# RWKV-7 chunk solve in a decoder trunk: two 64-row halves solved one after the other instead of one 128-row inverse

## What is computed

```python
def step(S, inp):
    r_t, w_t, k_t, v_t, kk_t, a_t = inp
    sa = jnp.einsum('bhij,bhj->bhi', S, -kk_t)
    S = (S * w_t[:, :, None, :]
         + sa[..., None] * (kk_t * a_t)[:, :, None, :]
         + v_t[..., None] * k_t[:, :, None, :])
    y = jnp.einsum('bhij,bhj->bhi', S, r_t)
    return S, y
```

## Time and profile before

| | us |
|---|---|
| median of 3 runs (1505.07 to 1511.18) | 1505.27 |
| the profiled execution, as a whole | 1507.26 |
| its span, first to last instruction | 1505.4 |
| TensorE busy | 1474.2 |
| VectorE (DVE) busy | 1242.6 |
| ScalarE (ACT) busy | 1009.8 |

### The profile page before, as it was taken

The page is one execution under the profiler, slowest core; times in us unless marked ns, Lnnn a source line. Parts: engine busy times, 40 slices in busy tenths (PEclk is TensorE's granted clock), DMA queues, the critical chain, the costliest instruction groups (busy, mean ns, idle before and its releaser), DMA issues.

```text
span 1505.4 us, 22041 instructions
## 1 busy us (share of the span) xinstructions
PE 1474.2 (98%) x8088; PEld 1226.9 (82%) x8088; DVE 1242.6 (83%) x1375; ACT 1009.8 (67%) x1157; POOL 22.2 (1%) x19
## 2 busy tenths in 40 slices
PE   8999999999899999999999999999999999999997
PEld 5888888799798588888888888888888888888885
DVE  3756666787885289999999999999999999999997
ACT  2544444663523178888888888888888878888885
POOL 0000000000000020000000000000000000000200
PEclk9999999999999999999999999999999999999998
DMA  9889553036405499999999999999999999999990
GB/s 361 326 271 301 175 168 112 1 117 217 141 2 178 174 322 372 395 392 395 396 392 396 394 368 388 390 365 383 394 366 373 393 386 362 395 380 362 349 369 28
DMA packets 206696, 453.57 MB, mean 301 GB/s; under 512 B 8881, under 2 KB 46257, under 8 KB 206386
## 3 DMA queue, kind: packets, MB, share of 16 engines
q1 hardware_dynamic: 203154, 446.12, 80.6%
q0 software_dynamic: 1280, 4.20, 1.1%
q10 hardware_dynamic: 2208, 2.50, 0.5%
HBM read 437.58 MB, written 23.60 MB: 306 GB/s over the span
## 4 chain that ended last, share of the span: by engine, by line
PE 92%; DVE 5%; ACT 2%; DMA 1%; issue 0%; DVEq 0%; ACTq 0%
PE psum L1591 20%; PE psum L1593 20%; PE psum L1592 20%; PE psum L2401 5%; PE psum L2404 3%; PE psum L902 2%; PE psum L2325 2%; PE psum L2365 2%; PE psum L2366 2%; PE psum L2367 2%; PE psum L600 2%; PE psum L1609 2%; PE psum L2318 1%; PE psum L696 1%; DVE time_mix_parts L1150 1%; PE psum L722 1%
## 5 line engine op out<-in xcount | busy, mean ns | idle before, releaser
L1799 DVE TENSOR_TENSOR w_lo<-ring,w_hi 128x1024 fp32r<-128x1024 f32 x672 | 811.0, 1224 | 63.5 <-ACT w_hi L1693 15.8
L1693 ACT ACTIVATE w_hi<-ring 128x1024 fp32r<-128x1024 f32 x672 | 711.3, 1062 | 172.5 <-PE psum L1593 172.4
L1591 PE MATMUL psum<-w_hi,xg_split 128*128 128x512 f32 x896 | 353.5, 395 | 0.3 <-DVE xg_split L1890 0.3
L1593 PE MATMUL psum<-w_lo,xg_split 128*128 128x512 f32 x896 | 349.4, 390 | 0.0
L1592 PE MATMUL psum<-w_hi,xg_split 128*128 128x512 f32 x896 | 348.8, 389 | 0.0
L1593 PEld LDWEIGHTS psum<-w_lo,xg_split 128*128 128x128 f32 x896 | 168.1, 188 | 35.8
L1591 PEld LDWEIGHTS psum<-w_hi,xg_split 128*128 128x128 f32 x896 | 168.3, 188 | 34.1 <-DVE xg_split L1890 0.6
L1592 PEld LDWEIGHTS psum<-w_hi,xg_split 128*128 128x128 f32 x896 | 168.4, 188 | 33.6
L1591 PE MATMUL psum<-w_hi,ht_split 128*128 128x512 f32 x448 | 176.0, 393 | 0.0
L1593 PE MATMUL psum<-w_lo,ht_split 128*128 128x512 f32 x448 | 174.6, 390 | 0.0
L1592 PE MATMUL psum<-w_hi,ht_split 128*128 128x512 f32 x448 | 174.4, 389 | 0.0
(11 more groups left out here) (370 smaller groups left out, 1488.7 us busy)
## 6 DMA issues: line engine op xcount, KB each, us to landing
ring<-o_moe_wg_dram SPq DMA_DIRECT2D x56, 2048.0 KB, 10.8
ring<-o_moe_wu_dram SPq DMA_DIRECT2D x56, 2048.0 KB, 11.3
ring<-o_moe_wd_dram SPq DMA_DIRECT2D x56, 2048.0 KB, 11.3
ring<-e_ffn_wg_dram SPq DMA_DIRECT2D x11, 1024.0 KB, 5.5
ring<-e_ffn_wu_dram SPq DMA_DIRECT2D x11, 1024.0 KB, 8.7
ring<-e_ffn_wd_dram SPq DMA_DIRECT2D x11, 1024.0 KB, 11.1
expert_rows<-work SPq DMA_DIRECT2D x1, 8192.0 KB, 27.9
ring<-e_w_in_dram SPq DMA_DIRECT2D x2, 2048.0 KB, 18.1
```

What stands on the lines that cost most here:

```text
L1591: nc.tensor.matmul(dst, x_hi, hi, start=first, stop=False)
L1593: return nc.tensor.matmul(dst, x_hi, lo, start=False, stop=last_)
L1693: nc.scalar.activation(w_hi[:, (4 * i + n) % 4, :], piece(i, n), ACT.Copy).then_inc(m_hi, 1)
L1799: V.tensor_tensor(w_lo[:, r, :], piece(i, n), w_hi[:, r, :].bitcast(F32), ALU.subtract).then_inc(m_lo, 1)
```

## The change

The third level goes. XT, Yv and Xv hold 64 columns for each head instead of 128: both 64x64 diagonal blocks, one in the upper and one in the lower 64 partitions. `turned` is now a product of XT with the even columns of the identity, for each half, and its result needs no picking when copied; banks 0 and 1 are used. The masks, the spread and the additions of the levels work on half the columns. U is found by forward substitution: `solved(c, pair, top)` gives the upper 64 tokens, ScalarE copies them, `carried` multiplies them with the coupling block of A, DVE adds that to the lower half of R, and `solved(c, pair, low)` gives the lower 64. `Us` moves to other memory, so the wait for rec_done 2 ahead of chunk 0's solve goes. `carried(0)` stands on DVE behind the last `recur(1, r)`. Pool's memset goes. Lines of functions shown above that are only removed are cut from the diff.

```diff
@@ -42,7 +42,7 @@
 CONST = {}
 CW = 0
 for _name, _w in (("ident", 128), ("ones", 128), ("upto", 128), ("before", 128), ("upto2", 128), ("heads", 128), ("iota", 128),
-                  ("cum", 256), ("blk16", 128), ("mask4", 64), ("mask5", 64), ("eye16", 16), ("par", 2), ("hsel", 142),
+                  ("cum", 256), ("blk16", 64), ("mask4", 32), ("mask5", 32), ("eye16", 16), ("par", 2), ("hsel", 142),
                   ("invcnt", 4 * T)):
...
     h4, h5 = np.arange(64)[None, :] // 16, np.arange(64)[None, :] // 32
-    put("mask4", (s // 32 == h4) & (s % 32 >= 16))
-    put("mask5", (s // 64 == h5) & (s % 64 >= 32))
+    put("mask4", (s % 64 // 32 == t32 // 16) & (s % 32 >= 16))
+    put("mask5", np.broadcast_to(s % 64 >= 32, (P, 32)))
...
-        Xv = [wu(3, 1024, 1024 * v).rearrange("p (g l t) -> p g l t", g=4, l=4) for v in range(2)]
-        Y6 = ru(13, 1024).rearrange("p (g n) -> p g n", g=4)
+        XT = [ru(4 + c, 1024).rearrange("p (g l t) -> p g l t", g=4, l=4) for c in range(2)]
+        Yv = [ru(6 + v, 1024).rearrange("p (g l t) -> p g l t", g=4, l=4) for v in range(2)]
+        Xv = [wu(3, 512, 1024 * v).rearrange("p (g l t) -> p g l t", g=4, l=4) for v in range(2)]
         Rs = ru(13, 1024, 1024).rearrange("p (g n) -> p g n", g=4)
         flatT = xnT[:, :, :].rearrange("p k t -> p (k t)")
         pick = flatT[:, 0:(B0 - 1) * P]
-        Us = flatT[:, 0:1024].rearrange("p (g n) -> p g n", g=4)
+        Us = ru(13, 1024).rearrange("p (g n) -> p g n", g=4)
         gsq = flatT[:, 1024:2048].rearrange("p (k t) -> p k t", k=KT)
         A1c = [r3(wu(2, 256, 512 * c), 16) for c in range(2)]
...
@@ -742,9 +734,52 @@
...
+                nc.tensor.transpose(psum[:, 2, 0:P], ident, ident)
+            pe.wait_ge(y_zero, 2)
+
+            tops = [slice(0, HD), slice(HD, P)]
+
+            def turned(c, v):
+                for pair in range(2):
+                    if v == 0:
+                        pe.wait_ge(x_full, 2 * c + pair + 1)
+                    else:
+                        pe.wait_ge(l_xd, lev(c, 0, pair))
+                    for gg, l, k, o, at in heads_of(pair):
+                        for hs in tops:
+                            even = ident[:, hs].rearrange("p (b h t) -> p b h t", h=2, t=B0 << v)[hs, :, 0, :]
+                            last = nc.tensor.matmul(psum[hs, pair, at // 2:at // 2 + 32], XT[c][hs, gg, l, :], even,
+                                                    start=True, stop=True)
+                    last.then_inc(l_tr, 1)
+
+            def level_Y(c, v):
+                for pair in range(2):
+                    pe.wait_ge(l_xe, lev(c, v, pair))
+                    if v == 0 and c == 1:
+                        pe.wait_ge(t_yc, pair + 1)
+                    for gg, l, k, o, at in heads_of(pair):
+                        for hs in tops:
+                            last = nc.tensor.matmul(psum[hs, 2 + pair, at // 2:at // 2 + 32], A_all[c][hs, gg, l, 0, hs],
+                                                    Xv[v][hs, gg, l, :], start=True, stop=True)
+                    last.then_inc(l_y, 1)
+
+            def level_X(c, v, pair):
+                pe.wait_ge(l_yd, lev(c, v, pair))
+                if v == 0 and c == 1:
+                    pe.wait_ge(t_sc, pair + 1)
+                for gg, l, k, o, at in heads_of(pair):
+                    odd = XT[c][:, gg, l, :].rearrange("p (b h t) -> p b h t", h=2, t=B0 << v)[:, :, 1, :]
+                    for hs in tops:
+                        last = nc.tensor.matmul(psum[hs, 4 + pair, at // 2:at // 2 + 32], Yv[v][hs, gg, l, :], odd[hs],
+                                                start=True, stop=True)
+                last.then_inc(l_xu, 1)
+
+            top, low = slice(0, HD), slice(HD, P)
+
             def right_side(c, pair):
                 pe.wait_ge(a_pm, 4 * c + 2 * pair + 2)
-                pe.wait_ge(l_xe, turned_at(c, 2, pair))
                 for gg, l, k, o, at in heads_of(pair):
                     dst = psum[:, pair, at:at + HD]
...
+            def solved(c, pair, rows):
+                if rows == top:
+                    pe.wait_ge(l_xd, lev(c, 1, pair))
+                    pe.wait_ge(t_rc, 2 * c + pair + 1)
+                else:
+                    pe.wait_ge(t_ca, 2 * c + pair + 1)
                 for gg, l, k, o, at in heads_of(pair):
...
+                    last = nc.tensor.matmul(psum[rows, 4 + pair, at:at + HD], XT[c][rows, gg, l, :],
+                                            Rs[rows, gg, HD * l:HD * l + HD], start=True, stop=True)
+                last.then_inc(t_u, 1)
+
+            def carried(c, pair):
+                pe.wait_ge(t_uc, 4 * c + pair + 1)
+                for gg, l, k, o, at in heads_of(pair):
+                    last = nc.tensor.matmul(psum[low, 4 + pair, at:at + HD], A_all[c][top, gg, l, 0, low],
+                                            Us[top, gg, HD * l:HD * l + HD], start=True, stop=True)
+                last.then_inc(t_c, 1)
 
             def outputs(c):
                 for pair in range(2):
...
+                    pe.wait_ge(t_uc, 4 * c + 2 + pair + 1)
                     pe.wait_ge(a_pm, 4 * c + 2 * pair + 2)
                     for gg, l, k, o, at in heads_of(pair):
                         dst = psum[o:o + HD, 2 + pair, (k % 4) * P:(k % 4 + 1) * P]
@@ -856,16 +839,16 @@
             block_rows(1, 2)
             level_X(0, 1, 0)
             level_X(0, 1, 1)
+            right_side(0, 0)
             block_rows(1, 3)
-            turned(0, 2)
-            right_side(0, 0)
-            pe.wait_ge(y_zero, 3)
-            top_Y(0)
+            right_side(0, 1)
+            solved(0, 0, top)
+            solved(0, 1, top)
             block_rows(1, 4)
-            right_side(0, 1)
-            top_X(0)
-            pe.wait_ge(rec_done, 2)
-            solved(0)
+            carried(0, 0)
+            carried(0, 1)
+            solved(0, 0, low)
+            solved(0, 1, low)
             outputs(0)
 
             turned(1, 0)
@@ -884,16 +867,17 @@
                 last = head_spread(gs[0], lambda j: psum[:, 6 + j // 4, (j % 4) * P:(j % 4 + 1) * P], j, HD)
             last.then_inc(gn_sp, 1)
             level_X(1, 1, 1)
-            turned(1, 2)
             right_side(1, 0)
-            top_Y(1)
             right_side(1, 1)
-            top_X(1)
-            solved(1)
+            solved(1, 0, top)
+            solved(1, 1, top)
+            carried(1, 0)
+            carried(1, 1)
+            solved(1, 0, low)
+            solved(1, 1, low)
             outputs(1)
 
             pe.wait_ge(t_yc, 4)
-            pe.wait_ge(l_x6, 4)
             gn_mean(1, 4)
             pe.wait_ge(gn_o, 1)
             pe.wait_ge(wo_in, 32)
@@ -1045,27 +1029,20 @@
 
             def right_side(c, pair):
                 act.wait_ge(t_r, 2 * c + pair + 1)
-                nc.scalar.activation(Rs[:, 2 * pair:2 * pair + 2, :], r3(psum[:, pair, :], 2),
-                                     ACT.Copy).then_inc(t_rc, 1)
+                nc.scalar.activation(Rs[:, 2 * pair:2 * pair + 2, :], r3(psum[:, pair, :], 2), ACT.Copy).then_inc(t_rc, 1)
+
+            def solved(c, pair, half):
+                rows = slice(HD * half, HD * half + HD)
+                act.wait_ge(t_u, 4 * c + 2 * half + pair + 1)
+                nc.scalar.activation(Us[rows, 2 * pair:2 * pair + 2, :], r3(psum[rows, 4 + pair, :], 2),
+                                     ACT.Copy).then_inc(t_uc, 1)
 
             def turned(c, v):
...
+                for pair in range(2):
+                    act.wait_ge(l_tr, lev(c, v, pair))
+                    dst = Xv[v][:, 2 * pair:2 * pair + 2, :, :].rearrange("p g l t -> p (g l t)")
+                    even = psum[:, pair, 0:256]
                     nc.scalar.activation(dst, even, ACT.Copy).then_inc(l_xe, 1)
...
 
             def outputs(c):
                 for pair in range(2):
@@ -1091,15 +1068,15 @@
             for s_ in range(8, 16):
                 copied(s_)
             for v in range(2):
-                nc.scalar.activation(r3(ru(6 + v), U // P), ident.unsqueeze(1).to_broadcast([P, U // P, P]), ACT.Copy,
+                nc.scalar.activation(r3(ru(6 + v, 1024), 8), ident.unsqueeze(1).to_broadcast([P, 8, P]), ACT.Copy,
                                      scale=0.0).then_inc(y_zero, 1)
             turned(0, 0)
             turned(0, 1)
...
+            for pair in range(2):
+                right_side(0, pair)
+            for half in range(2):
+                for pair in range(2):
+                    solved(0, pair, half)
             outputs(0)
 
             turned(1, 0)
@@ -1110,11 +1087,11 @@
             for k in range(KT):
                 last = nc.scalar.activation(gT[:, k, :], gT[:, k, :], ACT.Copy, scale=col("o_lnx_w", k))
             last.then_inc(gw_done, 1)
...
+            for pair in range(2):
+                right_side(1, pair)
+            for half in range(2):
+                for pair in range(2):
```

(73 more changed lines are left out.)

75 lines of the change are left out of this document (6 added, 69 removed).

## The result

| | median us | ratio to before, 95% interval |
|---|---|---|
| before | 1505.37 | |
| changed kernel | 1517.70 | 1.0076 [1.0062, 1.0091] |
| forecast | 1495.9 | |

The change makes the kernel 12.3 us slower where 9.4 us less were forecast. The profiled execution has a span of 1514.9 us. In the changed kernel line L753 is turned, L764 level_Y, L775 level_X, L785 and L788 right_side, L798 solved, L805 carried, L817 to L819 outputs.

A forecast was written before the change was run, and what follows sets the result against it. The prediction took TensorE to bound the kernel, the RWKV recurrence's chain lying on it nearly throughout. Gains of 4.7 us in chunk 0 and 4.7 in chunk 1 sum to 9.4, so 1505.27 becomes 1495.9, range 1491.5 to 1500.6.

The forecast's parts named there:

- first filler: Start of chunk 0: TensorE's 22 filler transposes start at 410.86, need about 2.5 us and end last; gain 1.06 us.
- forecast 9.66: Chunk 0 levels, turned(0,0) to the end of turned(0,1): 9.66 us of work against 10.51 before, gain 0.85.
- the price that no row showed: Solved and carried: each pass in one quarter of the array taken at 63 ns, 192 such passes in all.
- rival A: Quarter passes not overlapped, 138 ns each: 14.4 us more, 1510.3, slower than before; chance 0.04.
- rival C: Quarter passes at 31 ns, so a pair takes 0.5 us and the links rule: 1492.0; chance 0.08.
- The wait behind DVE: Chunk 0, ahead of solved low: TensorE waits about 0.76 us for DVE's addition, carried(0), behind the recurrence.
- Rival B: Handoffs between engines not hidden in substitution or levels, losing 2 to 5 us: 1498 to 1501; chance 0.22.
- a gain in front of the outputs of chunk 1 goes through whole: After 486.73 the chain is the same code, expert weight requests move earlier; first expert product to end stays 963 us.
- the reading that the idle times of TensorE in the scan are those behind ScalarE and DVE: Both chunks: chain nearly throughout on TensorE, idle only 0.98 us behind ScalarE, 0.64 and 0.83 behind level_X, one short.
- Rival D: TensorE's clock falls to the 1.2 GHz level for the 6 us of a substitution, losing about 3 us: 1499; chance 0.03.
- The sum: Chunk 0 gains 4.7 us and chunk 1 gains 4.7, together 9.4 us off 1505.27, giving 1495.9.

The follow-up runs named there:

- experiment 8: Changed kernel with output weights requested late and the last block rows of chunk 1 issued ahead of solved top of chunk 0: 1493.6 us, ratio 0.9914.
- Experiment 1: Changed kernel with one wait moved, so the output weights are requested behind the last level_X of chunk 1: 1497.16 us, ratio 0.9943.
- experiment 5: Kernel before, with TensorE made to wait ahead of turned(1,1) for two extra ScalarE copies: 1509.32 us, ratio 1.0015.
- experiment 6: Changed kernel, stall kept, with 32 extra 128x128 transposes behind turned(1,1): 1505.31 us.
- experiment 4: Changed kernel with 32 more quarter products (64 passes) behind the 22 filler transposes: 1518.53 us, ratio 1.0081.
- experiment 7: Changed kernel with the last block rows of chunk 1 issued ahead of solved top of chunk 0, instead of behind it: 1513.22 us.
- experiment 12: Kernel before with the forward substitution alone, level tiles still 128 columns wide and turned by 128x128 transposes: 1501.82 us, ratio 0.9965.

## Where the forecast was right and where it failed

**The durations held.** turned(0,0) starts 2.55 us behind the first filler (forecast 2.5). From there to the end of turned(0,1) it is 422.56 - 413.23 = 9.3, forecast 9.66. A quarter product, the price that no row showed, was taken at 63 ns a pass: 32 passes of the top solve take 2.0 us, so rivals A and C are out. The wait behind DVE was 0.73 for 0.76. In experiment 8, at full clock, it is 476.17 - 414.13 = 62.0 us from turned(0,0) to the outputs of chunk 1, against 477.3 - 413.4 = 63.9 less the 0.76 of idle time that its order removes. Rival B did not come either: between the pairs no idle time shows. That a gain in front of the outputs of chunk 1 goes through whole held too: from the first expert product to the end it is 963.4 us before and 962.3 after.

**The step that failed** is the reading that the idle times of TensorE in the scan are those behind ScalarE and DVE, so that a wait for TensorE's own instructions stood in no term of the sum. The change puts 64 passes where there were 16 transposes, four times in the scan (and narrower work instead of the third level), and I counted their time and not that they are instructions that must be fetched. The rows could not show a stall that is not there yet, but the transfer of 4 MB beside chunk 1 was in the trace before, and its effect on the fetch was no rival. The runs showed a stall of 1.68 us in its place and, behind it, the 1.2 GHz level for 37 us.

**Rival D**, the clock, had the right kind of cause and the wrong size, and this is the second step that failed. It was priced at 3 us and given 0.03, on the ground that the slices of the scan show full clock with idle times up to 1 us, and it took the low stretch to last one substitution of 6 us. Measured in chunk 1: 15.1 us up to the outputs, and 2.0 from there to the first expert product (552.63 - 496.44 = 56.2 us against 54.2 in experiments 1 and 8). In chunk 0: 3.5 us. In chunk 1 the change had also removed the 128x128 transposes that stood between the place of the stall and the outputs: before, there are some at 461.91 and once more behind the last level_X. In experiments 5 and 6, with such transposes behind the idle time, the low stretch lasted 6 to 7 us.

**The sum.** 9.4 us less were forecast and 12.3 more came, 21.7 apart. Found are 1.7 (stall), 15.1 + 2.0 (clock in chunk 1) and 3.5 (clock in chunk 0), 22.3 together. Experiment 1, the change without the stall, gives 8.5 with one low stretch left in it; experiment 8 gives 11.5, with the idle time gone and, in the profiled execution, without the low stretch that the kernel before has at 532, though with others at 410 and at 1489. So the gain that was forecast is there, by the mechanism that was forecast; what outweighed it was a late fetch and the clock.

## What to carry to other kernels

Price a change of many small products by its instructions too: where a transfer of megabytes runs beside them, look for idle times of TensorE that no semaphore explains, and move the transfer to a stretch with few instructions per microsecond. Look at the granted clock behind every new idle time: here one of 1.68 us cost some 19 us with narrow products behind it, and 32 transposes of 128x128 put there gave 12 us back, though they took 6 themselves. Moving one wait and one call was worth 24 us here, more than the whole rewriting.

## What was not expected of the hardware

- Beside a transfer at a DMA share of about 1.05, the fetch of TensorE's instructions came 1.4 to 1.7 us too late, in four kernels (the changed one, experiments 4, 6 and 7); without the transfer at that time, in none. Three kernels with the transfer there and the 16 one-pass transposes (before, experiments 5 and 12) have no stall.
- With TensorE busy all the time, the clock stayed at 1.2 GHz for 37 us. Up to the outputs nearly all of the products in it move 32 or 64 columns, 14 us of them with 128x128 weights; 16 with weights of 64x128 move 128 columns, for 2 us, and the clock stayed low there too. It came back about 4 us into the outputs (weights of 128x64, 128 columns moving), and in experiment 6 about 5 us into 128x128 transposes.
- 2.77 us of idle time instead of 0.83, with wide products behind it, took 3.7 us more, at the edge of what the runs can tell; 1.68 us with narrow products behind it took 16.8 up to the outputs.
